# 512-column operands of high and low part for nearly all products behind the scan, and modulation columns one a step

## The reference, cut to what matters

```python
# first block
u = rms_norm(x, ln1) * (1 + scale1) + shift1             # the mod vectors: silu(c) @ w_ada + b_ada, 6 x 1024
gl, cb, cc, cx, z, xbc, dt = split(u @ w_in)             # 2048, 1024, 1024, 1024, 2048, 4096, 32 columns
p_conv = (cb * causal_conv3(cc * cx)) @ w_conv_out
y = ssd_scan(xs * dt, dt * a, bs, cs) + d_skip * xs      # 32 heads; xs, bs, cs = silu(causal_conv4(xbc) + b)
y = group_norm(y * silu(z)) * ssm_norm_w
p_ssm = y @ w_ssm_out
g_conv, g_ssm = split(sigmoid(gl))
x = x + gate1 * ((g_conv * p_conv + g_ssm * p_ssm) @ w_o)
u2 = rms_norm(x, ln2) * (1 + scale2) + shift2
x = x + gate2 * (square(relu(u2 @ w_up)) @ w_down)       # 4096 hidden
x = rms_norm(x, final_norm)
# second block, with its own c_2 and mod vectors
h = rms_norm(x) * (1 + sc1) + sh1
fq, fk, fv, fg, dq, dk, dv = split(h @ w_in_2)           # 8 forget-gate heads, 4 differential heads of 2 x 64
mixed = concat(fox_attention(rms(fq), rms(fk), fv, log_sigmoid(fg + b_f)),
               rms(diff_attention(rms(dq), rms(dk), dv)) * 0.8)
x = x + g1 * (mixed @ w_out)
h2 = rms_norm(x) * (1 + sc2) + sh2
x = x + g2 * ((silu(h2 @ w_gate) * (h2 @ w_up)) @ w_down)   # 2816 hidden
```

## Time and profile before

| what | us |
|---|---|
| median of 3 runs | 1089.94 |
| lowest, highest | 1087.33, 1091.63 |
| the profiled execution | 1090.85 |
| its span | 1089.1 |
| TensorE, VectorE, ScalarE, GpSimd busy in it | 1014.0, 681.7, 505.7, 200.6 |

### The profile page before, as it was taken

One profiled execution on the slowest core, in us unless ns is written; L12 is line 12 of the kernel. 1 busy time (PEld: TensorE's weight loads), 2 busy tenths in 40 slices (PEclk: granted clock), 3 DMA queues, 4 the chain that ended last, 5 costly groups with the idle time before them and its releaser, 6 DMA issues.

```text
span 1089.1 us, 18542 instructions
## 1 busy us (share of the span) xinstructions
PE 1014.0 (93%) x7764; PEld 972.0 (89%) x7764; DVE 681.7 (63%) x919; ACT 505.7 (46%) x745; POOL 200.6 (18%) x230
## 2 busy tenths in 40 slices
PE   2499999999999989998999999599999889999998
PEld 1499999888899989998999999499998779999998
DVE  4878986655546557757888877645563457544442
ACT  3366553335555644435555333444454454444331
POOL 1200003322202431104444000011112221111100
PEclk9599999999999989998999999788999989999999
DMA  7744543333357647864877888523322246555451
GB/s 303 261 165 178 177 175 119 114 114 117 116 185 261 221 167 252 281 208 156 282 272 254 312 312 314 201 78 116 117 78 78 80 172 235 210 190 172 162 205 46
DMA packets 37011, 203.07 MB, mean 186 GB/s; under 512 B 5952, under 2 KB 6976, under 8 KB 18112
## 3 DMA queue, kind: packets, MB, share of 16 engines
q1 hardware_dynamic: 36928, 201.89, 52.8%
HBM read 200.82 MB, written 1.05 MB: 185 GB/s over the span
## 4 chain that ended last, share of the span: by engine, by line
PE 76%; DVE 9%; DMA 8%; ACT 4%; POOL 1%; issue 1%; SPq 0%; ACTq 0%; DVEq 0%
PE acc L839 63%; DMA maps<-in_ada_cols 6%; DVE w_lo L1067 2%; ACT w_hi L537 2%; DVE maps L1355 2%; DVE fr L1088 2%; PE m L872 2%; PE m L804 2%; PE m L863 1%; DMA xT<-in_x 1%; DVE cv L1238 1%; PE m L931 1%; PE m L918 1%; DVE raw L1116 1%; PE m L1009 1%
## 5 line engine op out<-in xcount | busy, mean ns | idle before, releaser
L1067 DVE TENSOR_TENSOR w_lo<-raw,w_hi 128x2048 fp32r<-128x2048 f32 (+2 forms) x144 | 323.8, 2249 | 188.4 <-ACT w_hi L537 188.4
L839 PE MATMUL acc<-uh,w_hi 128*128 128x256 f32 x1440 | 423.7, 294 | 12.8 <-POOL ul L463 12.7
L839 PE MATMUL acc<-ul,w_hi 128*128 128x256 f32 x1440 | 413.5, 287 | 0.0
L839 PE MATMUL acc<-uh,w_lo 128*128 128x256 f32 x1440 | 413.3, 287 | 0.0
L537 ACT ACTIVATE w_hi<-raw 128x2048 fp32r<-128x2048 f32 (+2 forms) x144 | 269.5, 1872 | 114.5 <-PE acc L839 72.0
L839 PEld LDWEIGHTS acc<-uh,w_hi 128*128 128x128 f32 x1440 | 281.8, 196 | 22.6 <-issue 17.8
L839 PEld LDWEIGHTS acc<-ul,w_hi 128*128 128x128 f32 x1440 | 282.9, 196 | 0.1
L839 PEld LDWEIGHTS acc<-uh,w_lo 128*128 128x128 f32 x1440 | 282.4, 196 | 0.0
L1355 DVE CUSTOM_DVE_ANT_0 maps<-maps,cact,par_all 128x1024 f32<-128x1024 f32 x80 | 116.9, 1463 | 20.7 <-DMA maps<-in_ada_cols 20.4
L839 PE MATMUL acc<-hidh,w_hi 128*128 128x256 f32 x432 | 122.7, 284 | 0.0
L839 PE MATMUL acc<-hidl,w_hi 128*128 128x256 f32 x432 | 121.6, 281 | 0.0
(11 more groups left out here) (227 smaller groups left out, 1449.7 us busy)
## 6 DMA issues: line engine op xcount, KB each, us to landing
raw<-in_tiles SPq DMA_DIRECT2D x138, 1024.0 KB, 4.9
maps<-in_ada_cols SPq DMA_DIRECT2D x80, 512.0 KB, 4.7
raw<-in_ada_tiles SPq DMA_DIRECT2D x8, 1024.0 KB, 7.2
raw<-in_rest SPq DMA_DIRECT2D x4, 768.0 KB, 5.4
cact<-in_c_rows SPq DMA_DIRECT2D x2, 512.0 KB, 5.4
xT<-in_x SPq DMA_DIRECT2D x1, 1024.0 KB, 13.2
out<-xT SPq DMA_DIRECT2D x8, 128.0 KB, 3.5
par_all<-in_params SPq DMA_DIRECT2D x1, 372.0 KB, 5.1
```

Of the source, the lines that this page charges most:

```text
L839: ins = pe.matmul(o, l, r, start=(s.k == 0 and i == 0 and not j), stop=(s.last and i == s.kts - 1 and j == 2))
L1067: dve.tensor_tensor(lo, raw_of(("step", n), s), hi.bitcast(F32), ALU.subtract).then_inc(S("lo_ready"), 1)
```

## The change

The high and low parts of an activation now lie side by side in one tensor (`u_x`, `yc_x` and so on, `[128, 2, blocks, 256]`), so that both can be one moving operand of 2 x 256 columns. For all kinds in `WIDE` the three products of a piece become two: weight high by (high, low) into all 512 columns of the bank, and weight low by high into the first 256. The bank then holds two halves that have to be added. For wo, dn, o2 and d2 (`DIRECT`) VectorE adds each half, times the gate, to x. For the others (`summed`) ScalarE copies the second half to SBUF (`correction`), VectorE adds the first half to it (`product_of_block`), and the step's own function is then taken from SBUF. dt, xbc, cc, cx, cb, the v's and fg stay as they are.

The columns get a buffer of their own and go one a step from step 35 to 116, with two steps left out before the 33rd, where SP loads c_2's row over c's in `cact` and ScalarE takes its silu. VectorE's waits for the columns are set later, to where each vector is needed.

```diff
--- before.py
+++ after.py
@@ -38,10 +38,15 @@
 NEG = -1.0e30
 LAM_INIT = 0.2
 NRAW, NHL, NACC, NF = 3, 3, 3, 4
+C2_GAP = 2
 NA0 = 2 * D // CW
...
+WIDE = ("gc", "co", "z", "gs", "so", "wo", "up", "dn", "dq", "dk", "fq", "fk", "o2", "gt", "u2", "d2")
+DIRECT = ("wo", "dn", "o2", "d2")
...
         self.tokens_out = kind in ("dt", "fv", "dv", "fg")
+        self.wide = kind in WIDE
+        self.summed = self.wide and kind not in DIRECT
+        self.w = None
...
-    g = 0
+    g = w = 0
     for s in steps:
         if s.k == 0:
-            s.g = g
+            s.g, s.w = g, w
             g += NB
+            w += NB * s.summed
         else:
-            s.g = prev.g
+            s.g, s.w = prev.g, prev.w
...
-    ACOL = NCOL - KB
+    C2COL = 48 - NB * NA0
     U0, W0 = start_of["up"], start_of["dn"]
-    col_step = [SCAN0 + 17 + m if m < W0 - SCAN0 - 17 else W0 + (m - (W0 - SCAN0 - 17)) // 2 if m < ACOL
-                else start_of["o2"] + 2 + m - ACOL for m in range(NCOL)]
-    col_at = {}
-    for m, n in enumerate(col_step):
-        col_at.setdefault(n, []).append(m)
-    assert col_step[40 - NB * NA0 - 1] + 2 < U0 and col_step[ACOL - 1] + 1 < start_of["dq"]
-
-    MOD1_AT, MOD4_AT = (col_step[c - NB * NA0 - 1] + 2 for c in (40, 96))
+    COL0 = SCAN0 + 17
+    col_step = [COL0 + m + (C2_GAP if m >= C2COL else 0) for m in range(NCOL)]
+    col_at = {n: [m] for m, n in enumerate(col_step)}
+    C2_AT = col_step[C2COL] - 1
+
+    def col_ready(c):
+
+        return col_step[c - NB * NA0 - 1] + 2
+
+    MOD1_AT = col_ready(40)
+    assert MOD1_AT <= U0 and col_ready(64) <= start_of["dq"] and col_ready(88) <= start_of["gt"]
...
-        uh = sb("uh", [P, KB, T], F32R)
-        ul = sb("ul", [P, KB, T], F32R)
+        u_x = sb("u_x", [P, 2, KB, T], F32R)
...
-        colw = maps[:, 0:2 * D].rearrange("p (s k) -> p s k", k=D)
+        colw = sb("colw", [P, 2, D])
...
+            if s.summed:
+                return "summed", s.w + nb + 1
...
                 if kind == "col":
-                    if n == 0:
-                        sp.wait_ge(S("pc"), N_CONST)
-                        sp.wait_ge(S("y_done"), HEADS)
-                    elif n == ACOL:
-                        sp.wait_ge(S("pv_done"), 12)
+                    if n == C2COL:
+                        sp.wait_ge(S("col_sum"), n)
+                        sp.dma_start(cact[:, :], a["c_rows"][1:2, :].to_broadcast([P, D])).then_inc(S("c2_in"), 16)
                     if n >= 2:
                         sp.wait_ge(S("col_sum"), n - 1)
                     sp.dma_start(colw[:, n % 2, :], a["ada_cols"][n]).then_inc(S(f"col_in{n % 2}"), 16)
...
-                if item == ("step", 1):
-                    sp.dma_start(cact[:, 1, :], a["c_rows"][1:2, :].to_broadcast([P, D])).then_inc(S("c2_in"), 16)
...
-                    if m == 0:
-                        act.wait_ge(S("col_sum"), ACOL)
...
+            def correction(s, nb, dst, wait=True):
+
+                bank = acc[(s.g + nb) % NACC]
+                if not s.wide:
+                    return bank[:, 0:T]
+                act.activation(dst, bank[:, T:2 * T], ACT.Copy).then_inc(S("correction"), 1)
+                if wait:
+                    act.wait_ge(S("summed"), s.w + nb + 1)
+                return dst
...
+                if n == C2_AT:
+                    act.wait_ge(S("c2_in"), 16)
+                    act.activation(cact[:, :], cact[:, :], ACT.Silu).then_inc(S("cact"), 1)
...
-                    bank = acc[(s.g + nb) % NACC]
-                    ps, free = bank[:, 0:T], S(drained(s, nb)[0])
-                    takes = s.last and s.kind in ("xbc", "cc", "gc", "z", "gs", "up", "dq", "dk", "fq", "fk", "fv",
-                                                  "dv", "gt")
+                    ps = acc[(s.g + nb) % NACC][:, 0:T]
+                    i = NB * s.j + nb
+                    takes = s.last and (s.summed or s.kind in ("xbc", "cc", "gc", "z", "gs", "up", "dq", "dk", "fq", "fk",
+                                                               "fv", "dv", "gt"))
                     if takes:
                         act.wait_ge(S("acc_ready"), s.g + nb + 1)
                     elif pending:
...
-                        act.activation(gt[:, nb, :], ps, ACT.Sigmoid).then_inc(free, 1)
+                        act.activation(gt[:, nb, :], correction(s, nb, gt[:, nb, :]), ACT.Sigmoid).then_inc(S("gate"), 1)
                     if s.kind == "z":
-                        i = NB * s.j + nb
                         if i >= 2:
                             act.wait_ge(S("yz_done"), i - 1)
                         else:
                             act.wait_ge(S("gate_used"), 8)
-                        act.activation(gt[:, nb, :], ps, ACT.Silu).then_inc(free, 1)
+                        act.activation(gt[:, nb, :], correction(s, nb, gt[:, nb, :]), ACT.Silu).then_inc(S("sz_done"), 1)
...
-                        act.activation(gt[:, nb, :], ps, ACT.Relu).then_inc(S("relu"), 1)
+                        if s.wide:
+                            correction(s, nb, gt[:, nb, :], False)
...
-                        act.activation(gt[:, nb, :], ps, ACT.Silu).then_inc(free, 1)
+                        act.activation(gt[:, nb, :], correction(s, nb, gt[:, nb, :]), ACT.Silu).then_inc(S("silu_g"), 1)
...
-                        act.activation(sq[:, 2 + nb, :], ps, ACT.Square).then_inc(S("qsq"), 1)
-                        act.activation(qk[:, b, :], ps, ACT.Copy).then_inc(free, 1)
+                        act.activation(sq[:, 2 + nb, :], correction(s, nb, qk[:, b, :]), ACT.Square).then_inc(S("qsq"), 1)
+                        if not s.wide:
+                            act.activation(qk[:, b, :], ps, ACT.Copy).then_inc(S("qk_raw"), 1)
+                    if s.kind == "co" and s.wide:
+                        correction(s, nb, mc[:, i, :], False)
+                    if s.kind == "so" and s.last:
+                        if i >= NB:
+                            act.wait_ge(S("f_ready"), MG + i - NB + 1)
+                        correction(s, nb, cv[:, nb, :], False)
+                    if s.kind == "u2" and s.wide:
+                        act.wait_ge(S("act_lo"), HID2 + i - NF + 1)
+                        correction(s, nb, fr[:, (HID2 + i) % NF, :], False)
...
-                    x_hi, x_lo = H[:, s.kt0 + kt, :], L[:, s.kt0 + kt, :]
+                    x = X[:, :, s.kt0 + kt, :]
+                    x_hi, x_lo = x[:, 0, :], x[:, 1, :]
                     wh, wl = w_hi[:, n % NHL, kt, 0:s.cols], w_lo[:, n % NHL, kt, 0:s.cols]
+                    head, tail = s.k == 0 and i == 0, s.last and i == s.kts - 1
+                    if s.wide:
+                        wh, wl = wh[:, nb * P:(nb + 1) * P], wl[:, nb * P:(nb + 1) * P]
+                        if i == 0:
+                            pe.matmul(out_[:, 0:2 * T], wh, x, start=head, stop=False)
+                        ins = pe.matmul(out_[:, 0:T], wl, x_hi, start=False, stop=False)
+                        if i:
+                            ins = pe.matmul(out_[:, 0:2 * T], wh, x, start=False, stop=tail)
+                        continue
...
+            def product_of_block(s, nb, dst=None):
+
+                ps = acc[(s.g + nb) % NACC][:, 0:T]
+                if not s.wide:
+                    dve.wait_ge(S("acc_ready"), s.g + nb + 1)
+                    return ps
+                dve.wait_ge(S("correction"), s.w + nb + 1)
+                dve.tensor_tensor(dst, ps, dst, ALU.add).then_inc(S("summed"), 1)
+                return dst
+
+            def gated(s, nb, dst, gate, done):
+
+                x = product_of_block(s, nb, dst)
+                if s.wide:
+                    dve.wait_ge(S("summed"), s.w + nb + 1)
+                return dve.tensor_tensor(dst, x, gate, ALU.mult).then_inc(S(done), 1)
...
-                if n == MOD4_AT:
+                if s.kind == "o2" and s.j == 0:
+                    dve.wait_ge(S("col_sum"), 72 - NB * NA0)
+                if s.kind == "d2" and s.j == 0 and s.k == 0:
                     dve.wait_ge(S("col_sum"), NCOL)
...
+                    i = NB * s.j + nb
+                    if s.kind in ("gc", "gs", "z", "gt") and s.wide:
+                        product_of_block(s, nb, gt[:, nb, :])
+                    if s.kind in ("dq", "dk", "fq", "fk") and s.wide:
+                        product_of_block(s, nb, qk[:, {"dq": 0, "dk": 4, "fq": 8, "fk": 12}[s.kind] + i, :])
...
                     if s.kind == "co":
-                        ready()
-                        dve.wait_ge(S("gate"), NB * s.j + nb + 1)
-                        dve.tensor_tensor(mc[:, NB * s.j + nb, :], ps, gt[:, nb, :], ALU.mult).then_inc(S("gate_used"), 1)
+                        dve.wait_ge(S("gate"), i + 1)
+                        gated(s, nb, mc[:, i, :], gt[:, nb, :], "gate_used")
...
+                        dve.wait_ge(S("gate"), 8 + i + 1)
+                        gated(s, nb, cv[:, nb, :], gt[:, nb, :], "gate_used")
```

(26 more changed lines are left out.)

68 lines of the change are left out of this document (24 added, 44 removed).

## The result

| what | us |
|---|---|
| after, median of 20 runs (lowest, highest) | 1090.05 (1087.84, 1094.34) |
| before, median of 20 runs beside them | 1088.94 (1086.62, 1091.97) |
| ratio after / before, 95% interval | 1.0020 (1.0011 to 1.0028) |
| the profiled execution of after, its span | 1090.0, 1088.3 |

A forecast was written before the change was run, and what follows sets the result against it. TensorE's issue pace was taken as the bound nearly everywhere, except dn, bound by column DMA and VectorE. Gains of 2.2 + 2.3 + 3.1 + 1.1 + 3.1 + 12.8 - 1.0 + 0 + 3.0 = 26.6 us gave 1064, range 1050 to 1088.

The forecast's parts named there:

- What a 512-column operand is worth: TensorE's products: a wide and narrow pair takes 216 + 120 = 336 ns, saving 24 ns on u, 20 elsewhere.
- first rival: The wide product costs 240 ns, no faster than two short ones; total 1090 us, chance 0.17.
- The second row of c ... Nothing: Loading c's second row behind column 31, with its silu moved out of xbc, costs nothing.
- up: Steps of up: VectorE, not TensorE, sets the step at 5.55 us against 5.76; 15 steps gain 3.1 us.
- gt and u2: Three pairs of steps at TensorE's 10.75 us, eight at 11.80: 126.7 against 126.7 before, nothing gained or lost.
- the ring: In gt and u2, ScalarE and VectorE wait in turn for splits and sums: 11.80 us a pair of steps.
- dn and its norm: 12.8 us gained: products 5.1, TensorE's waits for banks 2.9, earlier norm after the last product 4.8.
- gc/co, wo, d2: Gains forecast there: gc and co 2.2 us, wo together with o2 1.1, d2 3.0.
- The attention: 13 added columns and 16 sums cost 4 us against 8 x 0.38 = 3.0 gained: a loss of 1.0.
- z, so, o2: Gains forecast there: z 2.3 us after 0.8 charged, gs and so 3.1, wo and o2 together 1.1.
- The charge for the drains: Each summed block: ScalarE copy like 385 ns, VectorE addition like 421; wo, dn, o2, d2: a second 480 ns instruction.
- tight ring: Rival: 35 steps where ScalarE waits for VectorE's sum lose 1.0 us each; 1099 us, chance 0.08.

The follow-up runs named there:

- half_weights: c2_early with 64 weight columns instead of 128, for most narrow products in d2 and most wide ones in u2: 1085.94 us, single run.
- nodrain: c2_early with each block drained from its first half alone, without copies, sums or second additions: 1067.53 us, ratio 0.9807.
- widths: c2_early with most wide products cut to 256 columns in up, 320 in dn, 384 in gt, 448 in u2: 119, 146, 176, 202 ns each.
- contig: c2_early with high and low part of each block side by side, so the 512 columns are one run: 1082.16 us, one run.
- c2_early: The changed kernel with c's second row requested ahead of step 73's weights and its silu two steps later: 1084.42 us, ratio 0.9951.
- wide_oldcols: The 512-column products and their drains alone; columns, c's second row and its silu as in the kernel before: 1090.02 us, ratio 1.0009.

## Why the prediction was wrong

- **Step "What a 512-column operand is worth": failed, and it is the larger part.** It took 216 ns for the wide product, nearest to the plain float32 row, and argued that the narrow one's weights load beneath the long stream, so that the wide one would carry only 3 ns over 213. It carries 17 to 20, more than a short one's 12 or 13. The load beneath the stream is indeed hidden (`half_weights` in d2: 1.5 ns), but that took nothing off the wide one's pace. The pair is 350, not 336: 14 ns x 16 x some 68 steps bound by TensorE = 15 us. The two plain float32 products at 215 were another kind of product, and no row showed that a float32r one keeps their pace. The 13 ns over streaming at 256 columns was in hand: added once to 213 it gives 226 + 120 = 346, within 4 ns. The first rival's 240 was off by 6 to 9 on the other side; that its total, 1090, is what was measured is luck, as it had neither the 8 us of the late row nor dn's full gain. The Trainium skill, "TensorE: Matmul & The Clock Gate", section "Back-to-back issue gap", has 109 and 216 ns for 256 and 512 columns, 2.5 ns over streaming, as the gap of an isolated product; in the streams of the traces here it is 116 to 120 and 231 to 234, so a small excess for each instruction is there, but its size is 10 to 20 ns and not 2.5.
- **Step "The second row of c ... Nothing": failed, 8 us.** I named the order on SyncE and the silu's new place, and did not ask when the row's request stood against the silu: issue 544.47 plus 5.8 us of transfer, wanted at 542.9, with the copies of all later blocks behind it.
- **up:** without that step, the rest gained 1.9 of 3.1. TensorE's 5.59 a step bounds it, not VectorE's 5.55.
- **gt and u2: the ring was right**, 11.79 for 11.80, and there was no gain (the 1.1 come from the first gt step, of which less ran at half clock). Here too the pace was off: the pairs ahead of the ring took 11.19, not 10.75, but the forecast had three of them and there were five.
- **dn and its norm: right in mechanism**, 10.7 of 12.8. The stalls went (2.9, as forecast), the last step with the norm gave 6.5 (25.9 to 19.4 us) where 4.8 were forecast; the products gave 16 x 0.09 = 1.4 instead of 5.1. The norm's surplus of 1.7 covers part of the products' 3.7 that are missing, and that much of the agreement is luck.
- **gc/co, wo, d2:** gained 0.9, 1.0, 0.6. In gc/co only the pace was off; in wo and d2 the drains cost another 0.7 and 0.6 (against nodrain).
- **The attention:** the columns cost 0 of the 4 charged (with the sums); the drains of the q/k steps cost 2.4 (against nodrain). -1.0 became -3.4 in the trace of after, 1.6 of it at half clock (step 105, 30.0 us against 28.4).
- **z, so, o2:** the prediction charged 0.8 for the drains in z, nothing in gs and so, and 1.5 in wo and o2 together. Against nodrain they cost 0.9, 1.5 and 2.6 (o2 alone 1.9), and z lost another 1.5 at half clock.

The sum: the stages gained 1.3 us and not 26.6. Of the missing 25 some 15 are the pace, 8 the row; what is left is the sum of smaller misses both ways, above all z and so against the norm. The charge for the drains as a whole was not too small: the terms of the prediction gave away about 14 us for them (11.0 of these in gt/u2 and up), 18 with the attention's 4; the stages show 11, the medians 17. The tight ring did not come, and what would have shown it, rings over 11.8, is absent. The range ended at 1088 because the first rival's upper half was left out, and no case had a single bad step outside the rates.

## What to carry to other kernels

Merging two streamed products saves at most one instruction's excess over streaming (12 to 13 ns here; 6 to 10 were won). Take that excess from the stream that you have, add it once to the longer stream, and set against it what the drain of the second half costs, 11 to 17 us here against 14. Whoever moves a load past others must set its issue and its landing on the same clock as its first reader, and count all that stands behind that reader. In a ring of two engines put the short instruction that the other waits for ahead of the long one: here that order was worth 7 us of medians and 4 of the stages' sums, where the whole change gave none.

## What the runs showed of the hardware that I had not expected

- A float32r product of n columns, weights loaded for each, was followed after n/2.4 + 12 to 20 ns, from 256 (119) to 512 columns (230 to 233) in `widths`; halving the weight columns of one took 2 to 8 ns off a pair (`half_weights`). What these 12 to 20 ns consist of stays open.
- A 512-column operand from two places 8 or 32 blocks apart streams no slower than one run of columns (231 and 234 ns in `contig` and in after).
- A wait of TensorE of 2 us in z was followed by half clock in the trace of after (0.50 for 3.4 us, 1.5 us lost) and not in that of c2_early, with the same instructions ahead; single executions of one kernel lie up to 9 us apart (wide_oldcols 1086.44 to 1095.14), and a comparison of two profiled executions carries some microseconds of chance.
